# First window by single k-tiles: transposes in groups of one, two and four, splits of five halves in two pieces, shorter warm-up

## The reference, cut to what matters

```python
h = rmsnorm(x, norm_mix_g[l])                       # x: (1, 256, 2048)
proj = jnp.einsum('bsd,de->bse', h, w_in[l])        # w_in: (2048, 8192)
dq, dk, dv, mq, mk, mv, gate = jnp.split(proj, SPLITS, axis=-1)
```

## Time and profile before

| | |
|---|---|
| median of 3 runs | 576.2 us (576.13 to 576.22) |
| the profiled execution: its time | 576.07 us |
| its span from first to last instruction | 574.3 us |
| TensorE products (PE) busy | 564.9 us, 98% of the span |
| weight loads of TensorE (PEld) busy | 471.0 us, 82% |
| DVE busy, ACT busy | 421.2 us (73%), 406.8 us (71%) |
| DMA | 122.4 MB, mean 213 GB/s |
| granted clock of TensorE, mean | 0.996 |

### The profile page before, as it was taken

The page is one execution under the profiler, slowest core; times in us unless marked ns, Lnnn a source line. Parts: engine busy times, 40 slices in busy tenths (PEclk is TensorE's granted clock), DMA queues, the critical chain, the costliest instruction groups (busy, mean ns, idle before and its releaser), DMA issues.

```text
span 574.3 us, 8617 instructions
## 1 busy us (share of the span) xinstructions
PE 564.9 (98%) x2666; PEld 471.0 (82%) x2666; DVE 421.2 (73%) x704; ACT 406.8 (71%) x645; POOL 1.9 (0%) x25
## 2 busy tenths in 40 slices
PE   8999999999999999999999999999999999999994
PEld 7788888888888888888888888888888888888884
DVE  4668768778886876866756767668578787865875
ACT  5776966967868778776784784885598796854643
POOL 1000000000000000000000000000000000000000
PEclk9999999999999999999999999999999999999998
DMA  8998769668676776875975975979699987984303
GB/s 276 311 296 254 213 161 249 189 189 229 188 234 194 203 216 185 233 232 160 246 220 151 268 200 177 226 203 301 231 229 283 255 233 214 253 219 148 111 1 146
DMA packets 147500, 122.40 MB, mean 213 GB/s; under 512 B 63073, under 2 KB 129426, under 8 KB 146962
## 3 DMA queue, kind: packets, MB, share of 16 engines
q1 hardware_dynamic: 147442, 122.08, 74.7%
q10 hardware_dynamic: 32, 0.01, 0.0%
HBM read 106.06 MB, written 2.10 MB: 188 GB/s over the span
## 4 chain that ended last, share of the span: by engine, by line
PE 97%; DMA 1%; DVE 1%; ACT 0%; SPq 0%; issue 0%; ACTq 0%
PE ps L579 29%; PE ps L580 29%; PE ps L581 29%; PE ps L646 2%; PE ps L628 1%; PE ps L792 1%; PE ps L797 1%; PE ps L793 1%; DMA xs<-in_x 1%; PE ps L766 1%; PE ps L746 1%; PE ps L610 1%; PE ps L631 0%; PE ps L755 0%; DVE xs L1468 0%; PE ps L634 0%
## 5 line engine op out<-in xcount | busy, mean ns | idle before, releaser
L1152 DVE TENSOR_TENSOR w_lo<-w_raw,w_hi 128x1024 fp32r<-128x1024 f32 x187 | 227.5, 1222 | 109.5 <-ACT w_hi L828 107.2
L828 ACT ACTIVATE w_hi<-w_raw 128x1024 fp32r<-128x1024 f32 x187 | 197.0, 1058 | 87.1 <-PE ps L581 84.6
L579 PE MATMUL ps<-w_hi,aT 128*128 128x512 f32 x576 | 226.5, 393 | 0.0
L580 PE MATMUL ps<-w_lo,aT 128*128 128x512 f32 x576 | 224.3, 389 | 0.0
L581 PE MATMUL ps<-w_hi,aT 128*128 128x512 f32 x576 | 224.3, 389 | 0.0
L581 PEld LDWEIGHTS ps<-w_hi,aT 128*128 128x128 f32 x576 | 108.1, 188 | 22.8
L579 PEld LDWEIGHTS ps<-w_hi,aT 128*128 128x128 f32 x576 | 108.2, 188 | 22.6 <-issue 0.4
L580 PEld LDWEIGHTS ps<-w_lo,aT 128*128 128x128 f32 x576 | 108.2, 188 | 21.7
L579 PE MATMUL ps<-w_hi,yT_hi 128*128 128x512 f32 x144 | 56.2, 390 | 0.0
L581 PE MATMUL ps<-w_hi,yT_lo 128*128 128x512 f32 x144 | 56.0, 389 | 0.0
L580 PE MATMUL ps<-w_lo,yT_hi 128*128 128x512 f32 x144 | 56.0, 389 | 0.0
(11 more groups left out here) (187 smaller groups left out, 507.0 us busy)
## 6 DMA issues: line engine op xcount, KB each, us to landing
w_raw<-in_w_in SPq DMA_DIRECT2D x256, 256.0 KB, 3.3
w_raw<-in_w_out SPq DMA_DIRECT2D x64, 256.0 KB, 4.1
w_raw<-in_w_kv_mem SPq DMA_DIRECT2D x32, 256.0 KB, 4.1
w_raw<-in_w_q_mem SPq DMA_DIRECT2D x16, 256.0 KB, 3.0
w_raw<-in_w_o_mem SPq DMA_DIRECT2D x16, 256.0 KB, 3.5
mems<-in_mem SPq DMA_DIRECT2D x1, 2048.0 KB, 10.9
xs<-in_x SPq DMA_DIRECT2D x3, 512.0 KB, 7.8
w_raw<-in_final_g SPq DMA_DIRECT2D x1, 1024.0 KB, 4.4
```

The source lines that it names most:

```text
L579: pe.matmul(acc, hi[:, k0 + k, tok], w_hi[:, slot, k], start=first and k == 0, stop=False)
L580: pe.matmul(acc, hi[:, k0 + k, tok], w_lo[:, slot, k], start=False, stop=False)
L828: act.activation(w_hi[:, i % SPLITS], raw, ACT.Copy).then_inc(hi_made, 1)
L1152: dve.tensor_tensor(lo, w_raw[:, i % RAW], hi.bitcast(F32), ALU.subtract).then_inc(lo_made, 1)
```

## The change

The first window's start is rebuilt; the rest of the kernel stays.

- **Loads.** `x` comes in seven parts (128, 128, 256, 256, 256, 512, 512 columns). The first five halves come in three transfers each: k-tile 0 of the half as one of 256 KB with a semaphore of its own, k-tile 1 as two of 128 KB. `X_PART_BEFORE` places the parts of `x` ahead of halves 0, 1, 2, 3, 4 and 6 (part 1 is inside half 0).
- **Transposes** go by single k-tiles (`transpose_rows`), in PSUM banks 4 to 7 in turn: k-tiles 0 and 1 ahead of the first product, k-tile 2 behind k-tile 0's products, 3 behind 1, 4 and 5 behind 2, 6 and 7 behind 4, 8 to 11 behind 6, 12 to 15 behind 10.
- **Products** of the first eight halves (`first_half_group`) take all hi*hi products of a k-tile first, then wait for the `lo` parts.
- **Splits.** For the first five halves, ACT and DVE alternate per k-tile: rows, then 128x512 of weights. From half 5 on they split a whole half and then do the next k-tile's rows: half 5, rows 10, half 6, rows 11, half 7, rows 12, and on.
- **Sums of squares** go in half rows of 1024 columns: two between the splits of halves 7 to 9, two behind the split of half 10; `row_rms` moves from n == 6 to n == 8, behind one more reduction.
- **Warm-up**: `(3, 2)`.

```diff
-X_PARTS = ((0, 256), (256, 512), (512, 1024), (1024, 1536), (1536, 2048))
-WARM_UP = (5, 4, 2)
+X_PARTS = ((0, 128), (128, 256), (256, 512), (512, 768), (768, 1024), (1024, 1536), (1536, 2048))
+X_PART_BEFORE = (0, 2, 3, 4, 5, None, 6, None)
+SINGLE = 5
+ROWS_BEHIND = {0: (2,), 1: (3,), 2: (4, 5), 4: (6, 7), 6: (8, 9, 10, 11), 10: (12, 13, 14, 15)}
+WARM_UP = (3, 2)
...
+            def load_first_half(n):
+                sp.dma_start(w_raw[:, n, 0, :].rearrange("p (s c) -> p s c", c=2 * P),
+                             in_slabs[n][:, 0, 0:2, 0:2 * P]).then_inc(k_loaded[n], 16)
+                if n == 0:
+                    load_x(1)
+                for part, slab in enumerate(SLABS["diff", 0]):
+                    sp.dma_start(w_raw[:, n, 1, part * 2 * P:(part + 1) * 2 * P], in_slabs[n][:, 1, slab, 0:2 * P]
+                                 ).then_inc(half_loaded[n], 16)
...
+            def transpose_rows(k):
+                pe.wait_ge(x_loaded[X_PART_OF[k]], 16)
+                wait(pe, rows_lo, k - 3)
+                for t in range(NT):
+                    m = pe.transpose(ps[:, 4 + k % 4, t * P:(t + 1) * P], xs[:, t, k * P:(k + 1) * P], ident[:, :])
+                m.then_inc(rows_made, 1)
+            def first_half_group(n):
+                slot = n % SPLITS
+                for i in range(GK // 2):
+                    k = 2 * n + i
+                    first, last = k == 0, k == KO - 1
+                    pe.wait_ge(rows_hi, k + 1)
+                    pe.wait_ge(k_hi if i == 0 and n < SINGLE else hi_made, n + 1)
+                    for t in range(NT):
+                        pe.matmul(ps[:, t, :], aT_hi[:, k, t * P:(t + 1) * P], w_hi[:, slot, i], ...)
+                    pe.wait_ge(rows_lo, k + 1)
+                    pe.wait_ge(k_lo if i == 0 and n < SINGLE else lo_made, n + 1)
+                    for t in range(NT):
+                        pe.matmul(ps[:, t, :], aT_hi[:, k, t * P:(t + 1) * P], w_lo[:, slot, i], ...)
+                        m = pe.matmul(ps[:, t, :], aT_lo[:, k, t * P:(t + 1) * P], w_hi[:, slot, i], ...)
+                    if i == 1:
+                        m.then_inc(half_done, 1)
+                    for later in ROWS_BEHIND.get(k, ()):
+                        transpose_rows(later)
...
+            for n in range(SINGLE):
+                first_split_hi(n)
+            split_hi(5, 5, 0)
+            rows_out_hi(10)
+            split_hi(6, 6, 0)
+            rows_out_hi(11)
+            split_hi(7, 7, 0)
+            rows_out_hi(12)
+            sum_squares(0, 0)
+            rows_out_hi(13)
+            split_hi(8, 8, 0)
+            rows_out_hi(14)
+            sum_squares(1, 0)
+            rows_out_hi(15)
+            split_hi(9, 9, 0)
...
+            for n in range(SINGLE):
+                first_split_lo(n)
+            split_lo(5, 5)
+            rows_out_lo(10)
+            split_lo(6, 6)
+            rows_out_lo(11)
+            split_lo(7, 7)
+            rows_out_lo(12)
+            rows_out_lo(13)
+            split_lo(8, 8)
...
+            rows_out_lo(14)
+            rows_out_lo(15)
+            split_lo(9, 9)
```

More of the change, by code:

```diff
@@ L237, in program @@
         x_sq, at = columns(0, NT)
+        x_sq2, at = columns(at, NT, 2)
         x_ms, at = columns(at, NT)
@@ L292, in program @@
         half_loaded = [sem(f"half_loaded{s}") for s in range(RAW)]
-        first_hi = sem("first_hi")
-        first_lo = sem("first_lo")
+        k_loaded = [sem(f"k_loaded{n}") for n in range(SINGLE)]
+        k_hi = sem("k_hi")
+        k_lo = sem("k_lo")
         hi_made = sem("hi_made")
@@ L477, in turns @@
                     turn_probabilities(j - 1, n - P_TURN_AT[0])
-            load_x(0)
-            for n in range(PAIR_HALVES):
-                load_pair_half(DIFF, 0, 0, n)
-                if n in (0, 1, 3, 5):
-                    load_x((n + 1) // 2 + 1)
+            def load_first_half(n):
[6 more added lines that the diff above has]
+                                 ).then_inc(half_loaded[n], 16)
+            for n in range(PAIR_HALVES):
+                if n < 2 * NG and X_PART_BEFORE[n] is not None:
+                    load_x(X_PART_BEFORE[n])
+                if n < SINGLE:
+                    load_first_half(n)
+                else:
+                    load_pair_half(DIFF, 0, 0, n)
                 if n == 5:
@@ L565, in half_group @@
             def half_group(half, slot, banks, hi, lo, k0, first, last):
[L568 to L572, removed]
+                wait(pe, lo_made, half + 1)
                 for k in range(GK // 2):
-                    if first_half and k == 1:
-                        pe.wait_ge(lo_made, 1)
                     for t in range(NT):
@@ L589, in keep_busy @@
                     pe.matmul(ps[:, 2, 0:P], ident[:, :], ident[:, :], start=True, stop=True)
[L591 to L614, removed]
@@ L822, in split_hi, with rows_out_hi, first_split_hi @@
                 wait(act, half_done, half - behind + 1)
[L823 to L827, removed]
                 act.activation(w_hi[:, i % SPLITS], raw, ACT.Copy).then_inc(hi_made, 1)
[L830 to L840, removed]
+            def rows_out_hi(k):
+                act.wait_ge(rows_made, k + 1)
+                act.activation(aT_hi[:, k], ps[:, 4 + k % 4, 0:SEQ], ACT.Identity, scale=gainsT[:, k:k + 1]
+                               ).then_inc(rows_hi, 1)
+            def first_split_hi(n):
+                for i in range(GK // 2):
+                    rows_out_hi(2 * n + i)
+                    if i == 0:
+                        act.wait_ge(k_loaded[n], 16)
+                        wait(act, half_done, n - SPLITS + 1)
+                    else:
+                        act.wait_ge(half_loaded[n], 32)
+                    act.activation(w_hi[:, n % SPLITS, i], w_raw[:, n, i], ACT.Copy).then_inc((k_hi, hi_made)[i], 1)
             def split_turn(b, t):
@@ L1010, in _, with sum_squares @@
             act.wait_ge(gainsT_ready, 1)
[L1011 to L1029, removed]
+            def sum_squares(t, part):
+                loaded = range(5) if part == 0 else range(5, len(X_PARTS))
+                for n in loaded:
+                    act.wait_ge(x_loaded[n], 16)
+                cols = slice(part * DM // 2, (part + 1) * DM // 2)
+                act.activation(junk_row[:, 0:DM // 2], xs[:, t, cols], ACT.Square,
+                               accum_out=x_sq2[:, t, part:part + 1]).then_inc(x_summed, 1)
+                act.wait_ge(x_summed, 2 * part + t + 1)
+            for n in range(SINGLE):
[13 more added lines that the diff above has]
+            split_hi(9, 9, 0)
+            for n in range(2 * NG, PAIR_HALVES):
+                split_hi(n + 2, n + 2, 0)
+                if n == 8:
+                    sum_squares(0, 1)
+                    sum_squares(1, 1)
                 if n == 10:
```

90 lines of the change are left out of this document (39 added, 51 removed).

## The result

| kernel | median, us | runs | ratio to before, 95% interval |
|---|---|---|---|
| before | 576.2 | 7 (576.11 to 576.66) | |
| changed | 578.57 | 7 (577.52 to 579.34) | 1.0039 [1.0029, 1.0048] |

The change makes the kernel 2.4 us, 0.4%, slower. The forecast of 577.2 lies 1.4 us too low. Its wide range (573.6 to 579.2) holds the median; the range of the likeliest case (576.2 to 578.3) misses it by 0.3. The runs also spread more: over 1.8 us, where before spreads over 0.55.

The account below looks back on a forecast made before the run. TensorE, 98% busy, was to be held in half 6 by half 7's late weights: landing at 26.2 plus 8.3 starts half 8 at 34.5, 1.0 us later; 576.07 + 1.0 + 0.13 = 577.2 us, range 573.6 to 579.2.

Parts of the forecast that it names:

- likeliest case: Half 6 waits for half 7's weights: L from 25.2 to 27.3, time 576.2 to 578.3 us, chance 0.50.
- H8: Time at which TensorE starts half 8: 33.50 us before, forecast 34.5, 1.0 us later.
- L: Landing time of half 7's second weight transfer, for which ACT's split waits: taken as 26.2 us.
- rival 2: SP's issue queue delays half 7 by 2.2 us or more: L = 28.4, H8 = 36.7, time 579.4 us; chance 0.15.
- The first product: TensorE's first real product, forecast to start at 5.3 us, 2.9 us earlier than before.
- Rival 3: TensorE's clock stays low after early holes, costing 1.6 us: 575.4 us with half 7 early, chance 0.05; otherwise hidden.
- TensorE's own sum: First product, products, transposes and slow start on TensorE alone: H8 = 31.1 if nothing else binds, a gain of 2.4 us.
- rival 1: TensorE bound and faster: half 7 lands by 22.8, H8 = 31.1, time 573.8 us; chance 0.25.
- Rival 4: Split order on ACT and DVE without effect: L near 25.2, 576.2 us, no change; no separate chance given.
- cover of 0.6 us: `row_rms` result ready at L+13.1, wanted by TensorE behind half 9 at L+13.7: no new wait.

Follow-up runs that it names:

- after_again: The changed kernel measured a second time with no edit: 577.62 us, ratio 1.0020 to the kernel before.
- one_transfer: The changed kernel with k-tile 1 of the first five halves in one 256 KB transfer instead of two of 128 KB: 578.01 us, ratio 1.0036.
- rows_first: The changed kernel with the rows of k-tiles 12 to 15 ahead of the split of half 7 on ACT and DVE: 576.62 us, ratio 1.0005.
- lambda_late: The changed kernel with the four small lambda loads issued behind half 10 instead of ahead of half 7: 575.07 us, ratio 0.9982.
- busy_hole: The changed kernel with eight more identity products on TensorE behind half 5, filling the hole ahead of half 6: 577.14 us, ratio 1.0019.
- lambda_late_warm: The changed kernel with the four lambda loads behind half 10 and the longer warm-up (5, 4): 575.22 us, ratio 0.9982.
- order_alone: The kernel before with only the split of half 7 moved ahead of the rows of k-tiles 12 and 13: 576.79 us, ratio 1.0008.
- lambda_one: The changed kernel with one lambda load left ahead of half 7 and three behind half 10: 574.89 us, ratio 0.9975.
- both: The changed kernel with the lambda loads behind half 10 and rows 12 to 15 ahead of the split of half 7: 574.97 us, ratio 0.9978.

## Why the prediction was right

**The mechanism held.** "H8 = L + 8.3, and the edit pays nothing when L = 25.2." L and H8 are 26.56 and 34.88 in after_again and 26.06 and 34.37 in one_transfer: differences of 8.32 and 8.31. rows_first removes the hole with the order alone, lambda_late with the landing alone. The number is another matter. Two terms below, a later L and a low clock, each added more than 1 us to the profiled execution, whose 579.34 lies above even the wide range. That the median stayed inside is owed to the width of the range, which reached up to rival 2's time, and in part to luck.

**The first product** was put at 5.3 and starts at 5.48. The 2.7 us that this gives back are all in the changed kernel, and all lost again in half 6.

**L was mis-sized.** "I take half of the smallest delay, since most of the 8.9 us was spent queued: L = 26.2." It was 27.29 in the profiled execution and 26.56 in the second. In the profiled execution the issue was 1.13 later (1.2 was the smallest delay that I named; the issue of 2.12 us that I cited for it stands behind half 7's and could not delay it) and the transfer took 9.40 us, not less than 8.9. Bytes alone gave 25.6 and the issue alone 26.8; neither is the rule. What sets L is the dry stretch, and its depth differs from kernel to kernel and between two executions of one kernel. I had seen it in the earlier trace rows and read "a late issue can show". lambda_late shows that the four small loads make it, and one_transfer that five issues fewer don't end it. What makes its depth differ is not shown.

**The clock was a term that I left out of this case.** Rival 3 had it low at the start of the kernel; it fell behind the hole in half 6. In the profiled execution that took 1.2 us: H8 is 36.79 and L + 8.3 is 35.6. Worked out from the products, eight starts from 31.24 to 34.50 took 3.26 us instead of 8 x 0.227 = 1.8, 1.4 us more, of which k-tile 14's hole (0.3 us in after_again, 31.94 plus 0.23 to 32.47) took back a part. So the 3.3 us of the profiled execution are 2.1 (L + 8.3 - 33.5 at L = 27.3) and 1.2 of clock; the second one's are 1.4 (L = 26.56) and none. The medians are 2.4 and 1.3 us over before; five of the first measurement's seven runs and two of the second's eight have the low clock. That the hole causes the fall is what busy_hole speaks for, by its 11 runs beside one_transfer's three in six; why the same holes did not lower the clock in after_again (1.29 us) or in one_transfer (0.50 us) is open, that they are shorter is a guess. The Trainium skill (TensorE: Matmul & The Clock Gate, Part 1) says that the gate follows how busy TensorE has been of late. The fall behind the two holes agrees; its price here, 1.2 us, is this trace's.

**TensorE's own sum was 0.9 us short.** 31.1 was the sum, 32.04 is H8 in lambda_late, where nothing holds TensorE but 0.28 us at 7.64. Of the difference 0.2 is there at 7.64, when k-tile 0's products are done, and the rest lies between 7.64 and 32.04: 90 products at 0.227, 3.0 for 28 transposes and the gains' 0.2 make 23.6, where the timeline has 24.4. A pair of products or a product behind a transpose took 0.29 (10.00 to 10.29) instead of 0.23. So rival 1, had it come, would have been 574.7 and not 573.8, and no faster kernel than 574.9 was found.

**The rivals.** Rival 1's condition, half 7 in time, is what lambda_late makes true (23.09 at the latest), and it ends where this corrected price says. Rival 2 gave 579.4 and the profiled execution had 579.34, but for another reason: L was 27.3 and not 28.4, and the clock made up the rest. Rival 3's early holes cost little in lambda_late, by lambda_late_warm. How long the first products stay slow differs between executions, though: k-tile 0's six took 1.7 us in lambda_late, 2.2 in the changed kernel and 2.7 in busy_hole, where they follow each other at 0.42 to 0.43 us up to 8.03 (the column of the granted clock reads 1.00 there all the same). In the last two half 7's lateness covers it, as the prediction said. Rival 4, the order without effect, is answered by order_alone: H8 0.4 us later in its profile, and a median whose interval still touches no change.

**Bandwidth.** The Trainium skill (DMA: Bandwidth & Descriptors, Rules for kernel authors) says to coalesce small transfers and that under 64 KB one pays mostly overhead. I had weighed it for the 128 KB transfers that the change makes, and there one_transfer shows nothing clear. It bears on the four loads of 32 KB that the change left alone: their dry stretch agrees with it, and the one load that lambda_one leaves in place (339 to 363 GB/s around it) shows no cost.

**`row_rms` and the planes** brought no wait in the changed kernel, since time less H8 is the same as before to 0.02 us. I gave `row_rms` a cover of 0.6 us. In after_again its result is ready at 39.17 and TensorE's load takes it at 40.10, a cover of 0.9; in the profiled execution it is 1.9, since the low clock made TensorE later. In rows_first the cover is gone, and the load waits 0.53 us (L696 above). The planes' cover is thin too: ready at H8 + 4.2 they cost 0.2 us in "both", at H8 + 4.9 most of the 2.2 us in rows_first.

## What to carry to other kernels

When an in-order engine is to do "the split of a later block, then the rows of the current one", the current block inherits the landing time of the later one: check that transfer's landing against when the rows are needed, not when the split is. Several small loads back to back on the weights' queue are worth moving first; here that turned a loss of 0.4% into a gain of 0.2%, and it did nothing for the kernel whose order hid them. And where a hole lowers TensorE's clock in some runs and not in others, the median mixes two kinds of run: look at each run's mean granted clock before a term is fitted to it.

## What the runs showed of the hardware

- Four 32 KB broadcast loads in a row on SP's queue (15.45 to 17.34 in the changed kernel, 0.43 to 0.47 us each to issue) landed at about 20.9, 22.5, 23.8 and 26.0. From 20 to 23 us the DMA engines moved 60 to 109 GB/s (13 and 17 from 21 to 23 us in rows_first), while transfers of 256 KB stood issued: half 7's second was issued at 17.86 and landed at 27.26. Moved behind half 10, the same four were followed by 160 and 112 GB/s from 26 to 28 us. One such load did not do this (339 to 363 GB/s), and four with other transfers between them left 230 GB/s at the lowest. What in the engines does this is not shown.
- Behind holes of 2.02 and 0.56 us, in a stretch otherwise busy, the granted clock went to 0.50 (1.2 GHz) for some 3.4 us and cost 1.2 us; behind holes of 1.29 and 0.56 us, and of 0.50 and 0.56 us, it stayed at 1.00.
- Two executions of one kernel differed by 0.7 us in when ACT could start on the same transfer (27.29 and 26.56), issued at 17.86 and 17.9.
